# A two-stack transformer in fp32 on one core: the mixer's end reordered, first weight units prepared earlier, a two-layer loop written out

## What is computed

```
for l in range(DEPTH):                      # DEPTH = 2
    x = layer_norm(ALPHA * x + 0.5 * swiglu_ffn(x, ffn1_w_gu[l], ffn1_w_down[l]), ln1_g[l], ln1_b[l])
    x = layer_norm(ALPHA * x + hybrid_mixer(x, w_in[l], w_out[l], attn_sinks[l], ...), ln2_g[l], ln2_b[l])
    x = layer_norm(ALPHA * x + 0.5 * swiglu_ffn(x, ffn2_w_gu[l], ffn2_w_down[l]), ln3_g[l], ln3_b[l])

def hybrid_mixer(x, ...):                   # x @ w_in, then 8 heads of window attention, 8 of retention
    ...
    o = ((o - mu) * lax.rsqrt(var + GN_EPS)).reshape(B, S, H * D)      # per head, retention
    y_ret = silu(gate) * o
    return jnp.concatenate([y_attn, y_ret], axis=-1) @ w_out
```

## Time and profile before

| | |
|---|---|
| median of 3 runs | 2352.09 us (2348.13 to 2354.47) |
| the profiled execution | 2352.53 us, its span 2350.7 us |
| PE busy | 2042.0 us (87%) |
| DVE busy | 1195.2 us (51%) |
| ACT busy | 837.6 us (36%) |
| mean granted PE clock | 0.944 |
| expert stages, some 245 to 693 and 832 to 1258 us | DMA engines 0.98 and 0.99 busy |

### The profile page before, as it was taken

How to read it: one execution, slowest core, us unless ns; L and a number is a source line. 1 busy time by engine, 2 the same in 40 slices (tenths; PEclk the granted TensorE clock), 3 DMA queues, 4 the chain that set the end, 5 groups by cost and what they waited for, 6 DMA issues and landing times.

```text
span 2350.7 us, 47409 instructions
## 1 busy us (share of the span) xinstructions
PE 2042.0 (87%) x17878; PEld 1567.8 (67%) x17879; DVE 1195.2 (51%) x2424; ACT 837.6 (36%) x1644; POOL 27.5 (1%) x40
## 2 busy tenths in 40 slices
PE   7999888667779988766677999988999999988996
PEld 3568555344449855433445888877888888878886
DVE  3677422111126632111114766767667766767667
ACT  2232211011125411111113654546555654555555
POOL 0000000000000000000000000000001000000001
PEclk9999999888889999888898999999999999999998
DMA  9888799999996589999999545343556556343552
GB/s 392 334 298 339 325 430 432 432 430 431 432 422 257 224 361 432 431 431 432 431 431 363 199 147 192 108 165 121 170 150 203 180 159 199 109 144 120 191 148 79
DMA packets 273332, 662.59 MB, mean 282 GB/s; under 512 B 6064, under 2 KB 200624, under 8 KB 248112
## 3 DMA queue, kind: packets, MB, share of 16 engines
q1 hardware_dynamic: 273056, 658.82, 72.2%
q10 hardware_dynamic: 144, 2.03, 0.2%
HBM read 659.78 MB, written 1.05 MB: 281 GB/s over the span
## 4 chain that ended last, share of the span: by engine, by line
PE 66%; DMA 19%; DVE 6%; issue 4%; ACT 2%; SPq 1%; another core or an unknown queue 1%; ACTq 0%; DVEq 0%; PEldq 0%
PE ps L2266 19%; DMA ring<-in_moe_w_up 10%; PE ps L2271 10%; PE ps L1656 8%; DMA A<-in_moe_w_up 6%; PE ps L2598 4%; PE ps L1685 3%; DMA arena<-in_moe_w_up 2%; PE ps L1638 2%; PE ps L2763 2%; PE ps L1604 1%; PE ps L2063 1%; PE ps L2064 1%; PE ps L2065 1%
## 5 line engine op out<-in xcount | busy, mean ns | idle before, releaser
L2266 PE MATMUL ps<-XS,WS 128*128 128x512 f32 x1280 | 450.2, 397 | 11.2 <-DVE WS L2247 11.2
L2247 DVE TENSOR_TENSOR WS<-ring,WS 128x1024 fp32r<-128x1024 f32 (+1 forms) x276 | 328.8, 1194 | 184.7 <-ACT WS L2242 184.0
L2242 ACT CAST WS<-ring 128x1024 fp32r<-128x1024 f32 (+1 forms) x276 | 281.9, 1024 | 277.4 <-PE ps L2271 268.9
L2271 PE MATMUL ps<-XS,WS 128*128 128x256 f32 x1280 | 358.4, 280 | 0.0
L1933 DVE TENSOR_TENSOR RS<-RS,ps 64x256 f32<-64x256 f32 x70 | 29.6, 423 | 595.0 <-ACT RS L1750 595.0
L1656 PE MATMUL ps<-ring,RS 128*32 128x256 f32 x2176 | 237.7, 451 | 84.0 <-DMA ring<-in_moe_w_up 33.1
L2266 PEld LDWEIGHTS ps<-XS,WS 128*128 128x128 f32 x1280 | 241.9, 189 | 68.5 <-issue 12.0
L2271 PEld LDWEIGHTS ps<-XS,WS 128*128 128x128 f32 x1280 | 243.1, 190 | 0.0
L1656 PEld LDWEIGHTS ps<-ring,RS 128*32 128x32 f32 x2176 | 125.5, 129 | 148.3 <-issue 127.4
L2266 PE MATMUL ps<-HS,WS 128*128 128x512 f32 x616 | 216.4, 396 | 0.0
L1656 PE MATMUL ps<-arena,RS 128*32 128x256 f32 x1120 | 163.3, 456 | 54.0 <-DMA A<-in_moe_w_up 27.7
(11 more groups left out here) (387 smaller groups left out, 3525.7 us busy)
## 6 DMA issues: line engine op xcount, KB each, us to landing
ring<-in_ffn_w_gu SPq DMA_DIRECT2D x90, 1024.0 KB, 7.4
arena<-in_moe_w_down SPq DMA_DIRECT2D x32, 2048.0 KB, 47.7
ring<-in_moe_w_up SPq DMA_DIRECT2D x32, 2048.0 KB, 46.5
ring<-in_moe_w_down SPq DMA_DIRECT2D x32, 2048.0 KB, 46.8
ring<-in_moe_w_gate SPq DMA_DIRECT2D x32, 2048.0 KB, 46.0
ring<-in_w_mod SPq DMA_DIRECT2D x24, 2048.0 KB, 11.9
ring<-in_ffn_w_down SPq DMA_DIRECT2D x32, 1408.0 KB, 6.4
SPARE<-in_moe_w_gate SPq DMA_DIRECT2D x16, 2048.0 KB, 43.1
```

The costliest lines, as they stand in the source:

```text
L2242: L.inc(L.eng.copy(self.parts(u)[0], source), self.w_high)
L2247: L.inc(L.eng.tensor_tensor(wl, self.unit(u)[1], high(wh), ALU.subtract), self.w_split)
L2266: L.eng.matmul(ps[:, bank, :].rearrange("p (j t) -> p j t", j=2), wh[:, i, :], moving[:, :, k, :], start=k == 0, stop=False)
L2271: mm = L.eng.matmul(ps[:, bank, 0:TL], wl[:, i, :], moving[:, 0, k, :], start=False, stop=k == total - 1)
```

## The change

Five things change. (1) In the mixer's end DVE and ACT finish one tile before the next is begun, and PE's products for a tile no longer wait for the last unit (27) where they don't need it; the last pass runs over tile k = 7 alone. (2) The units 4 and 5 of a feed-forward (UNITS and UNITS + 1) are prepared inside the norm ahead of it. (3) The conv's first units are prepared at the end of the expert stage instead of in the norm; the buffers move in the arena for it. (4) At the second stack's start the raw parts are made inside the expert stage, before the squares on ACT; PE's sums of squares come after raw unit 0 and go to bank 6. (5) The loop over the two layers is written out: waits have constant values, and in the last layer lns[2] prepares nothing for a next one (`goes_on`).

```diff
@@ EarlyLayerNorm
+            def goes_on(self, L):
+                return not (self.raw and L.turn == LAYERS - 1)
...
@@ EarlyLayerNorm.act
-                stage.round_weights(L, UNITS - 1, later)
+                on = self.goes_on(L)
+                if on:
+                    stage.round_weights(L, UNITS - 1, later)
+                    if self.raw:
+                        stage.round_weights(L, UNITS, later)
...
+                if on:
+                    stream_high(L, self.done, KD - 1, self.split)
+                    if self.raw:
+                        stage.round_weights(L, UNITS + 1, later)
@@ EarlyLayerNorm.dve
-                    if k >= 2:
+                    if k >= 2 and on:
                         stream_low(L, k - 2, self.split)
+                    if k == 3 and on and self.raw:
+                        stage.split_weights(L, UNITS, later)
...
+                elif on:
+                    stage.split_weights(L, UNITS + 1, later)
@@ EarlyLayerNorm.pool
-                if self.raw:
+                if self.raw and self.goes_on(L):
                     L.wait(self.raw[1], KD)
@@ Norm.act
-                if self is norms[2]:
-                    for i in range(CONV_AHEAD):
-                        conv.round_weights(L, i)
+                if self is norms[4]:
+                    for u in range(1, UNITS + 1):
+                        ffns[0].round_weights(L, u)
@@ Norm.dve
-                if self is norms[2]:
-                    for i in range(CONV_AHEAD):
-                        conv.split_weights(L, i)
+                if self is norms[4]:
+                    L.inc(L.eng.memset(LN_MEAN, 0.0))
+                    for u in range(1, UNITS):
+                        ffns[0].split_weights(L, u)
                 L.wait(self.sums, 1)
...
                 if self is norms[4]:
-                    for k in range(KD):
-                        keep_raw_low(L, XT[:, k, 0:TL], vcol("final", KD)[:, k:k + 1], k, self.raw)
-                    L.inc(L.eng.memset(LN_MEAN, 0.0))
+                    ffns[0].split_weights(L, UNITS)
@@ LayerNorm.act
+                stage, later = self.next
+                stage.round_weights(L, UNITS, later)
                 L.wait(self.var, 1)
...
                 stream_high(L, self.done, KD - 1, self.split)
+                stage.round_weights(L, UNITS + 1, later)
@@ LayerNorm.dve
                 stage.split_weights(L, UNITS - 2, later)
+                stage.split_weights(L, UNITS - 1, later)
                 L.wait(self.sums, 1)
...
-                stage.split_weights(L, UNITS - 1, later)
+                stage.split_weights(L, UNITS, later)
                 L.wait(self.std, 1)
...
+                stage.split_weights(L, UNITS + 1, later)
@@ Moe.pe
-                self.next_norm.pe_sums(L, self.ADDED)
+                if self.next_norm is not norms[4]:
+                    self.next_norm.pe_sums(L, self.ADDED)
@@ Moe.act
+                if self.next_norm is norms[2]:
+                    conv.round_weights(L, 0)
                 if self.next_norm is norms[4]:
                     ffns[0].round_weights(L, 0)
+                    for k in range(KD):
+                        L.wait(self.x_added, self.ADDED.index(k) + 1)
+                        norms[4].act_raw(L, k)
...
+                if self.next_norm is norms[2]:
+                    for i in range(1, CONV_AHEAD):
+                        conv.round_weights(L, i)
@@ Moe.dve
+                if self.next_norm is norms[2]:
+                    for i in range(CONV_AHEAD):
+                        conv.split_weights(L, i)
                 if self.next_norm is norms[4]:
                     ffns[0].split_weights(L, 0)
+                    for k in range(KD):
+                        norms[4].dve_raw(L, k)
@@ Ffn.pe
+                    if u == 0 and not self.entry and L.turn == 0:
+                        norms[4].pe_sums(L, moes[1].ADDED)
@@ Ffn.act, Ffn.dve: for f == 0 units 4 and 5 are no longer rounded and split here
-                    round_weights(UNITS + 2 * f)
+                    if f:
+                        round_weights(UNITS + 2 * f)
...
@@ Mixer.pe
                 for k in (4, 5):
                     L.wait(self.y_split, k + 1)
-                    for m in range(KD):
+                    for m in range(6):
                         L.wait(self.w_split, B_UNIT + m // 2 + 1)
                         y_products(m, k)
                     if k == 4:
                         variance(3)
+                L.wait(self.w_split, B_UNIT + 4)
+                for k in (4, 5):
+                    for m in (6, 7):
+                        y_products(m, k)
+                L.wait(self.y_split, 7)
                 for m in range(KD):
-                    for k in (6, 7):
-                        L.wait(self.y_split, k + 1)
-                        mm = y_products(m, k)
+                    y_products(m, 6)
+                L.wait(self.y_split, 8)
+                for m in range(KD):
+                    mm = y_products(m, 7)
@@ every engine's program
-            with pe.Fori(0, LAYERS) as l:
-                L.turn = l
+            counted, stages = [(s, s.n) for s in Signal.made], counters["pe"]
+            for l in range(LAYERS):
+                L.start_turn(l, counted)
+                counters["pe"] = stages
```

More of the change, by code:

```diff
@@ L3196, in _ @@
             L.line, L.last = loop_line["act"], None
-            with act.Fori(0, LAYERS) as l:
-                L.turn = l
+            counted, stages = [(s, s.n) for s in Signal.made], counters["act"]
+            for l in range(LAYERS):
+                L.start_turn(l, counted)
+                counters["act"] = stages
                 for s in layer:
```

119 lines of the change are left out of this document (62 added, 57 removed).

## The result

The changed kernel takes **2321.95 us** (median of 4 runs, 2321.28 to 2324.01), the kernel before beside it 2353.28 (4 runs, 2348.13 to 2355.45): ratio of the runs taken side by side 0.9873, interval 0.9856 to 0.989. By the ratio that is 29.9 us less, 26 to 34 by its interval (the two medians lie 31.3 apart); forecast were 28.7 us and 2323.5. The profiled execution took 2322.09 us (span 2320.3), 30.4 less than the profiled one of before (2352.53).

What follows compares the result with a forecast made beforehand. Expert stage bound by DMA, conv and everything from 1272 us on by PE, so only seams pay: 9.0 + 8.2 + 3.4 - 1.0 + 4.4 + 4.7 = 28.7 us off 2352.1, said as 2323.5; range 2316 to 2333.

Steps and rivals of the forecast that it cites:

- The mixer's end: Mixer's end, both layers: the first gated tile is stored earlier and PE's 5.93 us wait goes; gain 4.5 us each, 9.0.
- The norm: Norm between mixer and second feed-forward, both layers: units 4 and 5 prepared earlier, unit 6 sooner; gain 4.1 us each, 8.2.
- The turn: Turn from layer 1 to 2: straight code removes PE's 3.95 us "issue" standstill, taken for the loop's jump; gain 3.4 us.
- The second stack's start: Start of the second stack: PE idle 7.7 us, sums behind the raw unit; loss 1.0 us, range gain 1.1 to loss 2.2.
- The conv: Conv's start: splits done before the variance, unit 3 reached earlier, passed on through the expert stage; gain 4.4 us.
- The end: Kernel's end: the last norm prepares nothing for a next layer, so the output's DMA starts earlier; gain 4.7 us.
- Half level in new places: Rival: PE's half clock returns behind new short gaps; four 4.4 us stretches cost 9 us, giving 2332.5 us; chance 0.19.
- Turn: Rival: the gap between layers isn't the loop's; gain 1.3 instead of 3.4 us, giving 2325.6 us; chance 0.07.
- conv: Rival: the conv's gain is lost in the expert stage because its DMA stream doesn't shift; 2328 us; chance 0.06.
- mixer's order: Rival: ACT answers late, last tile stored as before, only the half level's 2.3 us goes, twice; 2328 us; chance 0.05.
- late instruction fetch: Rival: the second layer's new code is fetched too late for PE; all 28.7 us gone or slower, 2365 at 7 ns; chance 0.03.

Runs made afterwards that it cites:

- the filled run: Changed kernel with the mixer's end as before, plus twelve filler matmul calls in PE's standstill there; 2337.17 us, 0.9929 of the kernel before.

## Why the prediction was right

**What bounds it.** Right: the change paid at the seams alone, and the stages between them are as long as before, but for lengths that differ between executions of one program.

**The mixer's end** (4.5 each). The first addition comes 4.6 us earlier against the feed-forward's end (134.49 and 139.06 us behind it). The single times fit as well: gaps of 0.61, 0.43, 0.15 for 0.9, 0.5, 0.2, and the additions pace what follows. Three steps inside the sum were off. I gave 2.3 of the 4.5 to the half level; a us of it loses 0.44 us and not half a us, and in the kernel before it cost 1.7 and 1.6 (from the first gated product to the first addition 10.73 and 10.68 us, against 0.22 + 8.82 = 9.04 at full clock by the filled run). The waiting itself was the larger part. I let PE's new passes carry part of it: undone alone they are worth 0.4 to 0.5. And the last two tiles' times don't follow from my own terms: 3.5 us a tile and 1.2 for unit 27 give 84.7 and 88.2, where I wrote 84.2 and 87.5. The trace has 84.0 and 87.3 on the clock of before, since DVE has four operations and then two behind the last two reciprocals, not five; the written times were right, but not by the terms given.

**The norm** (4.1 each). From the first raw unit to unit 6: 27.4 and 27.3 before, 23.3 twice after, 4.1 and 3.9. The waits moved to units 5 and 6, one us each, as forecast.

**The turn** (3.4). 3.85. That the pieces with "issue" at their end are the loop's is shown by the run that changes only the loop. The rule of the Trainium skill that stood as a rival (Advanced Engine Details and Errata, Control Flow Timing, 108 and 51 ns for its branches) doesn't account for them: here 3.95 and 3.42 us went with the loop. What in a loop's turn takes so long, the jump or the register operations at its head, no run shows.

**The second stack's start** (-1.0). -0.84, with the standstill of 7.90 us (forecast 7.7) and unit 6 31.9 us behind the expert stage's end. It is the one part of the change that loses; two runs show that putting the sums first there wins 3.1 and 4.0 us at that seam.

**The conv** (4.4). 4.2, and the DMA-bound stage behind it passes it on.

**The end** (4.7). 4.96, and 5.03 when undone.

**What was not in the sum.** 1.25 us up to the first expert stage's end and 2.11 in the second one for, 2.40 in the feed-forwards against: together 1.0 us for the change, and none of it shown to be the change's. The range took one feed-forward's cadence in on its lower side alone, and with 46 units instead of 68, 2.3 us where a whole feed-forward differs by 2.7; the same draw could have gone the other way, up to four times 2.7 us. That the sum of these lengths came to 1.0 us in the one execution profiled is luck. In the medians much of it cancels.

**The rivals.** Half level in new places: on the additions once in 18 passes, 2.9 us for a stretch of 6.6; for four of them at once the 0.19 was high. Turn, conv, mixer's order, late instruction fetch: each ruled out by a run.

## What to carry to other kernels

Look at what stands on the slow engine between a tile's last input and its last output, and cut that chain to one tile's work; order on the engine that waits (here PE, 2.19 us of standstill for a cost of 0.5) mattered little here, because PE catches up before the last tile. A standstill removed alone can come back one seam on, as at the turn: follow the next late producer before counting the gain. And where parts of a few us are to be judged, compare distances between fixed instructions within a trace; the total of one execution carries draws that are as large.

## What the runs showed of the hardware

- One and the same sequence of matmuls at full clock and with no idle time has two cadences, 2.773 and 2.827 us for a weight unit, fixed for the gate and up part of one feed-forward and open again for the next: 2.7 us for a whole feed-forward.
- The half-level stretch behind a standstill falls on more or less of the work in the same code: 3.6 and 5.4 us behind standstills of 5.85 us, at a cost of 1.6 and 2.4. Matmuls of 256 columns, each with its own weights, follow each other every 0.213 us at the half level and every 0.119 at full clock, so a us at the half level loses 0.44 us.
- Such a stretch, 3.4 us long, stood behind a standstill of 2.19 us in both layers of one run, and once in 18 passes one of 6.6 us stood behind pauses of at most 1.16 us.
- A filler call on 512 fp32 columns leaves two records and takes 0.87 us, not one of 0.45: count the calls in the code before pricing a row of the profile.
